# Attention inside a two-layer block: the values become the stationary operand, and the result comes out transposed

## The reference

```python
s_win = jnp.einsum('bnqgrd,bnkgd->bngrqk', qb, kw) * scale
s_win = jnp.where(valid[None, :, None, None], s_win, NEG_INF)
s_ctx = jnp.einsum('bnqgrd,bcgd->bngrqc', qb, k_ctx) * scale
p = softmax(concatenate([s_win, s_ctx, s_sink], -1))
o = einsum(p[..., :kw_len], vw) + einsum(p[..., kw_len:-1], v_ctx)
x = x + g1 * (jnp.concatenate([att, ret, cnv], axis=-1) @ w_out[l])
```

## Time and profile before

| What | Value |
|---|---|
| Median of three runs | 1928.89 us |
| Time of the profiled execution | 1920.56 us |
| Its span, first to last instruction | 1918.8 us |
| PE busy | 1819.8 us (95%) |
| PEld busy | 1482.6 us (77%) |
| DVE busy | 1340.3 us (70%) |
| ACT busy | 1053.6 us (55%) |
| Mean granted PE clock | 0.98 |
| Attention rounds of layer 0 | from about 174 to 266 us |
| Attention rounds of layer 1 | from about 787 to 843 us |

### The profile page before, as it was taken

One profiled execution on the slowest core, in us unless ns is written; L12 is line 12 of the kernel. 1 busy time (PEld: TensorE's weight loads), 2 busy tenths in 40 slices (PEclk: granted clock), 3 DMA queues, 4 the chain that ended last, 5 costly groups with the idle time before them and its releaser, 6 DMA issues.

```text
span 1918.8 us, 23772 instructions
## 1 busy us (share of the span) xinstructions
PE 1819.8 (95%) x8964; PEld 1482.6 (77%) x8964; DVE 1340.3 (70%) x1280; ACT 1053.6 (55%) x1009; POOL 119.8 (6%) x126
## 2 busy tenths in 40 slices
PE   4999999999999999887999999999999999999997
PEld 1886477888888878566788887888888888888885
DVE  2477745432432357755889888889988898889886
ACT  2333643322122244455677667777767777677773
POOL 1032800000000012310000000000000000000000
PEclk9999899999999999998999999999999999999999
DMA  8334833522433134643999998999989999899993
GB/s 290 104 110 145 306 120 88 143 83 82 110 89 104 40 115 140 230 174 132 342 337 377 363 369 306 371 352 362 391 307 363 357 370 378 304 364 363 360 375 141
DMA packets 245911, 472.85 MB, mean 246 GB/s; under 512 B 10546, under 2 KB 60564, under 8 KB 245804
## 3 DMA queue, kind: packets, MB, share of 16 engines
q1 hardware_dynamic: 241712, 468.14, 68.5%
q10 hardware_dynamic: 4092, 3.20, 0.5%
HBM read 470.26 MB, written 1.05 MB: 246 GB/s over the span
## 4 chain that ended last, share of the span: by engine, by line
PE 79%; DVE 7%; DMA 5%; ACT 4%; issue 2%; POOL 2%; SPq 0%; DVEq 0%; ACTq 0%; POOLq 0%
PE bank L543 23%; PE bank L545 23%; PE bank L544 23%; DMA raw<-in_moe_w_gate_dram 2%; DVE parts L1707 2%; PE bank L1047 2%; DMA raw<-in_ada_w_dram 1%; PE bank L561 1%; ACT parts L1410 1%; DMA raw<-in_moe_w_up_dram 1%; PE bank L1102 1%; POOL gb L1663 1%; PE bank L790 1%; DVE parts L1692 1%; ACT parts L1271 1%
## 5 line engine op out<-in xcount | busy, mean ns | idle before, releaser
L1707 DVE TENSOR_TENSOR parts<-raw,parts 128x2048 fp32r<-128x2048 f32 x336 | 764.5, 2288 | 100.8 <-ACT parts L1410 99.7
L1410 ACT ACTIVATE parts<-raw 128x2048 fp32r<-128x2048 f32 x336 | 642.9, 1919 | 236.9 <-DMA raw<-in_moe_w_up_dram 77.0
L543 PE MATMUL bank<-parts,XEr 128*128 128x512 f32 x896 | 355.5, 397 | 7.6 <-DVE parts L1707 5.5
L545 PE MATMUL bank<-parts,XEr 128*128 128x512 f32 x896 | 349.7, 390 | 0.0
L544 PE MATMUL bank<-parts,XEr 128*128 128x512 f32 x896 | 349.1, 390 | 0.0
L1271 ACT ACTIVATE parts<-raw 128x2048 fp32r<-128x2048 f32 (+1 forms) x62 | 113.2, 1831 | 273.4 <-PE bank L545 252.5
L1692 DVE TENSOR_TENSOR parts<-raw,parts 128x2048 fp32r<-128x2048 f32 (+1 forms) x62 | 135.7, 2193 | 143.0 <-ACT parts L1271 142.7
L543 PEld LDWEIGHTS bank<-parts,XEr 128*128 128x128 f32 x896 | 168.6, 188 | 44.5 <-issue 6.2
L545 PEld LDWEIGHTS bank<-parts,XEr 128*128 128x128 f32 x896 | 168.3, 188 | 36.2
L544 PEld LDWEIGHTS bank<-parts,XEr 128*128 128x128 f32 x896 | 168.6, 188 | 33.2
L543 PE MATMUL bank<-parts,HTr 128*128 128x512 f32 x448 | 174.8, 390 | 0.0
(11 more groups left out here) (245 smaller groups left out, 2296.4 us busy)
## 6 DMA issues: line engine op xcount, KB each, us to landing
raw<-in_moe_w_gate_dram SPq DMA_DIRECT2D x112, 1024.0 KB, 6.6
raw<-in_moe_w_up_dram SPq DMA_DIRECT2D x112, 1024.0 KB, 6.6
raw<-in_moe_w_down_dram SPq DMA_DIRECT2D x112, 1024.0 KB, 6.3
raw<-in_ada_w_dram SPq DMA_DIRECT2D x28, 1024.0 KB, 7.9
more<-in_ada_w_dram SPq DMA_DIRECT2D x20, 1024.0 KB, 7.5
raw<-in_w_in_dram SPq DMA_DIRECT2D x12, 1024.0 KB, 5.1
raw<-in_ffn_w_gate_dram SPq DMA_DIRECT2D x22, 512.0 KB, 4.0
raw<-in_ffn_w_up_dram SPq DMA_DIRECT2D x22, 512.0 KB, 5.4
```

Of the source, the lines that this page charges most:

```text
L543: nc.tensor.matmul(out, st[0], mv[0], start=start, stop=False)
L545: return nc.tensor.matmul(out, st[1], mv[0], start=False, stop=stop)
L1410: nc.scalar.activation(parts[:, n % PARTS, 0, :], raw[:, r, :], ACT.Copy).then_inc(hi_ready, 1)
L1707: return nc.vector.tensor_tensor(out, a, b, op)
```

## The change

`values` now takes a pair of heads at once. The stationary operand is the 64 columns of values of one group, the moving one the 128 columns of the transposed probabilities. Group 0 writes partitions 0 to 63 of `OB` and group 1 partitions 64 to 127, alternating from key block to key block. The result has head dims on partitions and tokens on columns, which is what the output projection needs, so `turn_attended` goes away. The row sums still have tokens on partitions. `spread_sums` therefore multiplies each head's inverted sums, broadcast to 64 columns, with the identity (eight f32 matmuls for a tile) into an `AB` bank; ACT copies this to `proj` (`sums_out`), and DVE multiplies `OB` by it (`normalise`).

The order moves with it. `spread_sums` stands on PE in rounds 5, 9, 13 and 17, between `values` and the modulation products. `sums_out` stands on ACT in the following round, behind its exponentials, and `normalise` on DVE in that round, behind the negated maximum (for the last tile in round 17). In rounds 6, 10 and 14 PE does the modulation products ahead of `values`. `attended_high` and `mix_low` read the tile from `proj`, no longer from a bank. The rows of the first half of `w_out` are loaded in another order, by two loads of 64 partitions for each item instead of one of 128. The diff, with indentation cut:

```diff
--- before.py
+++ after.py
@@ -317,6 +317,7 @@
 sarg_ready, esink_ready = sem("sink_arg_ready"), sem("sink_exp_ready")
+recip_ready = sem("row_sums_inverted")
 att_done, att_read = sem("attention_products"), sem("attention_evacuated")
@@ -367,6 +368,10 @@
+def evacuated(layer, i):
+    return layer * (NT + 1) + i + 2
 def attention_of(layer):
@@ -427,10 +432,12 @@
     for h in range(2):
-        for k0, k1 in HALVES:
-            split_item([cols(io["w_out"][layer], h * SLICE, (h + 1) * SLICE, k0, k1)],
-                       k1 - k0, SLICE, n % 2, (n + layer) % 2)
-            n += 1
+        w = io["w_out"][layer][:, h * SLICE:(h + 1) * SLICE]
+        groups = [w[256 * g:256 * g + 256, :].rearrange("(r p) n -> p r n", p=HEAD_DIM) for g in range(KV_HEADS)]
+        split_item(groups, KT // 2, SLICE, n % 2, (n + layer) % 2)
+        n += 1
+        split_item([cols(w, 0, SLICE, KT // 2, KT)], KT // 2, SLICE, n % 2, (n + layer) % 2)
+        n += 1
     if layer == 0:
@@ -750,12 +757,18 @@
-    def turn_attended(layer, t):
-        b = open_mix(layer, t, 0)
-        for i in range(4):
-            c = C_Q + i * P
-            mm = nc.tensor.transpose(b[:, i * P:(i + 1) * P], proj[:, t, c:c + P], ident)
+    def spread_sums(layer, i):
+        t = order_of(layer)[i]
+        mixed[layer, t, 0] = len(mixed) + 1
+        b = open_a(("sums", layer, t))
+        after(recip_ready)
+        turn = i % 2
+        for r in range(4):
+            for g in range(KV_HEADS):
+                head = g * 4 + r
+                mm = nc.tensor.matmul(b[64 * g:64 * g + 64, r * P:(r + 1) * P],
+                                      rsum[:, turn, head:head + 1].broadcast_to([P, HEAD_DIM]), ident, start=True, stop=True)
         mm.then_inc(a_full, 1)
@@ -779,18 +792,19 @@
-        def values(n):
-            t, r, g = its[n]
-            head = g * 4 + r
-            if n % 8 == 0 and n:
+        def values(m):
+            t, r, _ = its[2 * m]
+            if m % 4 == 0 and m:
                 after(att_read)
-            pe.wait_ge(a_done, job[("probs", layer, n)] + 1)
             first = 0 if t < TT else TT
+            pe.wait_ge(a_done, job[("probs", layer, 2 * m + 1)] + 1)
             for kb in range(first, NT):
-                mm = nc.tensor.matmul(OB[:, head * 64:(head + 1) * 64], PT[:, n % 4, kb * P:(kb + 1) * P],
-                                      proj[:, kb, C_V + 64 * g:C_V + 64 * g + 64],
-                                      start=(kb == first), stop=(kb == NT - 1))
-            mm.then_inc(att_done, 1)
+                for g in range(KV_HEADS):
+                    mm = nc.tensor.matmul(OB[64 * g:64 * g + 64, r * P:(r + 1) * P], proj[:, kb, C_V + 64 * g:C_V + 64 * g + 64],
+                                          PT[:, (2 * m + g) % 4, kb * P:(kb + 1) * P],
+                                          start=(kb == first), stop=(kb == NT - 1))
+                    if kb == NT - 1:
+                        mm.then_inc(att_done, 1)
@@ -801,11 +815,13 @@
             if m >= 2:
-                values(2 * m - 4)
-                values(2 * m - 3)
-            if m % 4 == 2 and 6 <= m < last:
-                turn_attended(layer, order_of(layer)[m // 4 - 1])
-            if m < last:
+                if m % 4 == 2 and m < last:
+                    for _ in range(ADA_ITEMS[layer][m]):
+                        ada_product()
+                values(m - 2)
+            if m % 4 == 1 and m >= 5:
+                spread_sums(layer, m // 4 - 1)
+            if m < last and m % 4 != 2:
                 for _ in range(ADA_ITEMS[layer][m]):
@@ -865,7 +881,6 @@
                             after(att_read)
-                            turn_attended(layer, tiles[-1])
                         if i == len(tiles) // 2 - 1:
@@ -1208,6 +1223,9 @@
         for j, src in enumerate(srcs):
+            if src.shape[0] == HEAD_DIM:
+                sp.dma_start(dst[j * HEAD_DIM:(j + 1) * HEAD_DIM, :, :], src).then_inc(raw_loaded[s], 16)
+                continue
             sp.dma_start(dst[:, :, j * part_w:(j + 1) * part_w], src).then_inc(raw_loaded[s], 16)
@@ -1353,6 +1371,13 @@
+    def attended_high(layer, i):
+        t = order_of(layer)[i]
+        act.wait_ge(att_read, evacuated(layer, i))
+        nc.scalar.activation(hTr[:, 0, 0:4, t * P:(t + 1) * P],
+                             proj[:, t, C_Q:C_RQ].rearrange("p (k n) -> p k n", k=4), ACT.Copy).then_inc(mix_hi, 1)
     def mix_high(t, half):
@@ -1371,6 +1396,9 @@
             ins.then_inc(product, 1)
+        def sums_out(i):
+            copy_out(proj[:, order_of(layer)[i], C_Q:C_RQ], take()[:, :])
@@ -1387,6 +1415,8 @@
                     nc.scalar.activation(esink[:, turn, :], esink[:, turn, :], ACT.Exp).then_inc(esink_ready, 1)
+            if m % 4 == 2 and m >= 6:
+                sums_out(m // 4 - 1)
             if m >= 1:
@@ -1397,9 +1427,10 @@
             if m % 4 == 2 and 6 <= m < last:
-                mix_high(order_of(layer)[m // 4 - 1], 0)
+                attended_high(layer, m // 4 - 1)
             if m == last - 1:
                 split_to(first["out", layer] + 2)
+        sums_out(last // 4 - 1)
@@ -1549,7 +1580,7 @@
         nc.scalar.activation(gates, CV[:, 0:nt, :], ACT.Silu).then_inc(act_mix, 1)
-        mix_high(order_of(layer)[-1], 0)
+        attended_high(layer, nt - 1)
         for t in order_of(layer):
@@ -1990,6 +2021,13 @@
         rest, norm = readout(layer), conv_norm(layer)
+        def normalise(i):
+            tile = order_of(layer)[i]
+            dve.wait_ge(att_done, base + 8 * i + 8)
+            dve.wait_ge(a_done, job[("sums", layer, tile)] + 1)
+            tt(proj[:, tile, C_Q:C_RQ], OB[:, :], proj[:, tile, C_Q:C_RQ], ALU.mult).then_inc(att_read, 1)
         dve.wait_ge(conv_gone, CONV_OUTS * (layer + 1))
@@ -2012,6 +2050,8 @@
                     tt(esink[:, turn, :], negm[:, turn, :], sink[:, :], ALU.add).then_inc(sarg_ready, 1)
+                if m % 4 == 2 and m >= 6:
+                    normalise(m // 4 - 1)
                 for c in taps_in(layer, m):
@@ -2027,20 +2067,18 @@
                 turn = (m // 4 - 1) % 2
-                tile = order_of(layer)[m // 4 - 1]
                 after(esink_ready)
                 step(tt(rsum[:, turn, :], rsum[:, turn, :], esink[:, turn, :], ALU.add))
-                step(nc.vector.reciprocal(rsum[:, turn, :], rsum[:, turn, :]))
-                dve.wait_ge(att_done, base + 2 * m - 2)
-                tt(proj[:, tile, C_Q:C_RQ].rearrange("p (h d) -> p h d", d=HEAD_DIM), OB[:, :].rearrange("p (h d) -> p h d", d=HEAD_DIM),
-                   per_group(rsum[:, turn, :], HEAD_DIM), ALU.mult).then_inc(att_read, 1)
+                nc.vector.reciprocal(rsum[:, turn, :], rsum[:, turn, :]).then_inc(recip_ready, 1)
+            if m == last + 1:
+                normalise(last // 4 - 1)
         assert next(rest, None) is None and next(norm, None) is None
     def mix_low(layer, t, half):
-        b = a_bank[full[("mix", layer, t, half)]]
+        b = a_bank[full[("mix", layer, t, half)]] if half else proj[:, t, C_Q:C_RQ]
         k, tok = slice(4 * half, 4 * half + 4), slice(t * P, (t + 1) * P)
         dve.wait_ge(mix_hi, mixed[layer, t, half])
-        tt(hTr[:, 1, k, tok], b[:, :].rearrange("p (k n) -> p k n", k=4), hTr_f[:, 0, k, tok], ALU.subtract)\
+        tt(hTr[:, 1, k, tok], (b[:, :] if half else b).rearrange("p (k n) -> p k n", k=4), hTr_f[:, 0, k, tok], ALU.subtract)\
             .then_inc(mix_lo, 1)
```

## The result

| Kernel | Median, us | Runs | Ratio to the kernel before, same chip |
|---|---|---|---|
| before | 1928.95 | 4 | |
| changed | 1950.05 (1945.37 to 1958.62) | 4 | 1.0111 [1.0087, 1.0135] |
| changed, second time | 1951.77 (1943.32 to 1956.85) | 6 | 1.0128 [1.0100, 1.0156] |

The change makes the kernel slower by 21.1 us in the first comparison. I had said slower, by 9.3, with 1947 as the upper end of the range: the sign held and so did the waits as the main cause, but the sum came to less than half of what was measured. The profiled execution of the changed kernel took 1949.91 us (span 1948.0, granted clock 0.973), that of before 1920.56 (1918.8, 0.980).

What follows compares the result with a forecast made beforehand. PE was taken as busiest, but its new waits for DVE and ACT as deciding: layer 0 +7.2 and layer 1 +2.1 make +9.3 us, put on the median 1928.9: 1938 us, range 1926 to 1947.

Steps and rivals of the forecast that it cites:

- the waits: PE's new waits for DVE and ACT around `spread_sums` and `values` decide: slower, 1933 to 1944 us, chance 0.58.
- A pair of values at 0.97: `values` of two heads on PE: 8 slots of 0.12 us, 0.97 us in place of 1.93.
- Round 11 with `turn_conv` at 5.69: Layer 0, round 11, no new wait: PE's round takes 5.11 + 0.58 us, before 6.25.
- The second meeting: Rounds 6, 10, 14: `values` wait for `normalise`, which ends 5.5 us into the round.
- Round 13 at 4.68 + 1.17 + 1.86: Layer 0, round 13: reciprocal at 4.68 us, then spreading 1.17 and two modulation products 1.86, before round 14.
- The 9.3 us to the maxima of round 15: Layer 0, from round 14's start: DVE does `normalise` until 5.5 us, then `conv_norm`, 3.81 us, before these maxima.
- Layer 1 at +2.1: Layer 1's attention: new waits in rounds 5 and 6 and the tail make it 2.1 us slower.
- The rival of halves that don't overlap: `values` and spreadings on PE take 16 slots, their column halves not running side by side: 1949 us, chance 0.07.
- PE's saving: Rival: the waits cost nothing and PE's shorter work decides, about -5 us, 1924 us, chance 0.13.
- "nothing": Rival: over the whole kernel waits and savings cancel, 1925 to 1933 us, chance 0.13.
- The clock: Rival: stalls in rounds 10, 13, 14 bring PE to half clock, at most +5 us, 1943 us, chance 0.07.
- the first meeting: Rounds 5, 9, 13: `spread_sums` waits for the reciprocal, holding up modulation products and next scores; 0.6 us idle in round 9.

Runs made afterwards that it cites:

- the one with the low half moved: Changed kernel with `mix_low` of layer 0's first attended tile moved from round 7 to round 11: 1948.98 us, ratio 1.0108.
- the fillers: Changed kernel with idle f32 matmuls in layer 0 ahead of the four spreadings and the transposes of rounds 7 to 9: 1946.87 us, ratio 1.0094.
- new form alone: Changed kernel without spreading, `sums_out` or multiplication; DVE copies `OB` out, modulation products behind `values` again, division left out: 1927.81 us, ratio 1.0016.
- neither meeting: Changed kernel, DVE copying `OB` out, spreading one round later, multiplying from the sums' bank, products behind `values`, no ACT copy: 1935.34 us, ratio 1.0034.
- fillers and low half: Changed kernel with both the idle matmuls in layer 0 and the first tile's `mix_low` moved to round 11: 1941.58 us, ratio 1.0065.

## Why the prediction was right in sign and wrong in size

**What held.** A pair of values at 0.97: 1.02. Round 11 with `turn_conv` at 5.69: 5.55. The second meeting 5.5 us into the round: 5.8 in round 10 and 5.55 in round 14. Round 13 at 4.68 + 1.17 + 1.86 = 7.71: 7.72, with PE idle ahead of the spreading for 1.66 us (1.6 expected; in round 9 it was 1.90 in place of 0.6). The 9.3 us to the maxima of round 15, behind `conv_norm`: 9.36. Layer 1 at +2.1: +2.9 on average, which a scatter of 3.8 us between two profiles of one kernel neither confirms nor denies. The rival of halves that don't overlap is out (1.51 when they are made not to), PE's saving doesn't decide, and neither does "nothing".

The Trainium skill ("TensorEngine Tiling (Array Packing)", Performance Considerations) recommends the swap for a moving side of 64 columns, and the Overview of the same page gives up to 2x for it. For the products the trace agrees, 1.93 to 1.02; for the kernel, that form alone gave a ratio of 1.0016.

**Where it failed: layer 0 up to round 10**, where the sum had round 10 at 227.3, 53.3 us after round 0. It came at 58.7, 5.4 later. Of the 11.8 us by which the sum fell short of the medians, 6.9 are layer 0's up to the projection (14.1 and not 7.2). The rest lies in layer 1 (0.8) and in parts for which the sum had nothing: about 1 to 3 us in the dense part and 2.5 to 6 in the experts'; its cause is open. Up to round 10 two steps failed.

*"`attended_high` and `mix_low` do the same size from SBUF as from a bank: nothing."* For `mix_low` it is 4.02 - 2.33 = 1.7 us, when GpSimd works at the same time. From 206.58 to 222.11 GpSimd added without a break, nine additions of 1.73 us. In the kernel before, `mix_low` from the bank took 0.68 in the middle of this and the next instruction 1.69; without `mix_low` that next one took 2.29 alone; with it read from SBUF, 1.77 and 2.29. So the bank version cost DVE nothing: it ran while the next one would have had to wait. The Trainium skill states the rule that I should have weighed ("SBUF — State Buffer", section "SBUF: two separate sides"): a DVE instruction with two SBUF inputs and a GpSimd instruction that reads SBUF exclude each other for a whole instruction. The trace agrees: the excess of 1.09 us is less than one addition of 1.73, and in round 11, with GpSimd idle, it is gone.

GpSimd in the changed kernel, its additions of that stretch in one row:

```profile
206.58 15.53 POOL L1694 TENSOR_TENSOR gb<-gb,QK 128x512 f32<-128x512 f32 x9
```

*The clock.* I priced it as a rival at 0.07 and took full speed for the sum: "the new stalls in rounds 10, 13 and 14". I looked for it behind the stalls that I had found in layer 0's second half, and not behind the first meeting in rounds 5 and 9, where PE also stands still for 2.94 and 1.90 us first. In round 5 it cost 3.77 - 2.02 = 1.75 us from the spreading to the scores of round 6 (changed kernel against the one with the low half moved, which had full speed there), and the readout got all of it: it starts 35.4 us after round 0, and 33.6 at full speed (34.05 in before). In round 9 it cost (1.90 + 3.57) - (1.17 + 1.86) = 2.4 us, with no cover.

The ledger of the 5.4 us: clock in round 5 +1.8, clock in round 9 +2.4, low half from SBUF +1.7, the negated maximum of round 9 +0.5 (1.23 against 0.71), a rest of 0.3; against them the readout's slip of 0.9, which without the clock would have been -0.4, so -1.3. The experiments have the low half at 1.8 and the clock of round 9 at 2.4, after the fillers' own time. Round 5 gained nothing by the fillers (round 6 at 30.5 us with them, at 30.2 without), as the clock had already been at half in round 1 there and the reciprocal came 1.4 us later.

A third term was too small. From round 10 to the projection the sum had +5.1 and the trace has +6.6. Up to the maxima of round 15 it was right (+4.4 against +4.3); the tail came to +2.3 where I had +0.7. The last spreading starts 0.15 us after the end of the reciprocal and takes 1.90 at half clock, and only then can the projection start. In the kernel before it started 0.25 us ahead of the end of the reciprocal. The 1.1 us that I took off, for the transposes saved and for the low clock used up, can only come behind this point, where the next stretch has +0.5 and -1.0. The timeline of PE in the changed kernel, end of layer 0's attention, and the first matmul of the projection in before:

```profile
275.49 1.09 PE L803 MATMUL bank<-PT,proj 128*64 128x128 f32 x16 [3.37 <-ACT PT L1352]
278.25 1.97 PE L770 MATMUL bank<-const,rsum 128*64 128x128 f32 x16 [1.67 <-DVE rsum L2072]
280.15 0.80 PE L550 MATMUL bank<-parts,hTr 128*128 128x512 f32 x1
```
```profile
266.97 0.79 PE L543 MATMUL bank<-parts,hTr 128*128 128x512 f32 x1
```

**What stays open.** The 18.6 and 19.2 us at the gather leave 2.5 to 6 of the measured difference (21.1 and 25.3 between medians) for the experts' part. That the profiles show 11 to 14 there is partly which executions were profiled: those of before took 8.4 and 4.7 us less than the median, those of the changed kernel 0.1 less and 5.1 more. The windows of its first 100 us, in before and in the changed kernel:

```profile
895.60:995.60 100.00, 93.00 (x424) 77.64 (x425) 85.47 (x73) 66.23 (x49) 0.00 (x0) 0.96 0.87 321
```
```profile
913.30:1013.30 100.00, 93.37 (x412) 77.97 (x413) 82.55 (x71) 63.36 (x48) 0.00 (x0) 0.92 0.85 307
```

At 0.92 in place of 0.96, 93 us of PE time would be some 4 us longer, an estimate from these two rows. The difference isn't the changed kernel's alone. Here are stretches with the same code in all versions (one profile each, before and changed two), and the mean granted clock of all executions:

| Version | dense part up to layer 1, us | experts' part, us | clock in its first 100 us | clock, all executions |
|---|---|---|---|---|
| before | 498.3, 498.3 | 1023.2, 1023.1 | 0.96, 0.96 | 0.977 |
| new form alone | 499.4 | 1027.5 | 0.93 | 0.974 |
| neither meeting | 501.4 | 1033.4 | 0.92 | 0.973 |
| changed | 499.5, 501.3 | 1034.7, 1037.4 | 0.92, 0.93 | 0.971 |
| changed, fillers | 502.1 | 1028.6 | 0.94 | 0.975 |
| fillers and low half | 502.1 | 1024.7 | 0.94 | 0.975 |

Every version with the new form is slower there than both profiles of before, also the one without any new wait. Why the clock differs, when the code is the same, no run tells, and no experiment on it was made; and the clock's share, some 4 us, doesn't cover the 11 to 14 either. This is also the open part of the 6 us of the version without meetings.

## What to carry to other kernels

A shorter matmul form is worth what the round's longest chain lets through: here 16 us of PE time came to 2 in layer 0 and to nothing at the end. Before moving a division behind a matmul, count the handovers: with the next scores queued behind a matmul that awaits a reciprocal, the kernel took 9 us more than with the same matmul placed one round later. When a sum has a new PE wait in a critical round, price what follows it at half clock as well, and when an operand moves from a bank to SBUF, look at what GpSimd does at that moment.

## What the runs showed of the hardware that was not expected

Idle matmuls can make the stretch behind a wait shorter: with them, PE got from the end of round 9's reciprocal to round 10 in 3.4 us and not 5.6. They didn't make this kernel measurably faster (1.0094 [1.0077, 1.0111] against 1.0111 [1.0087, 1.0135]), and by round 12 the gain was gone: the clock had fallen at the next wait without a filler, of 2.52 us in round 10. Where the granted clock falls depends on small shifts: in two versions with the same work up to round 6 it fell to 0.83 from 186 to 196 or to 0.68 from 196 to 202, 1.7 us apart at round 6. In round 1, where no edit acts, it was at half in the kernel before and in the version with fillers (0.51 and 0.50), and at full speed in the changed kernel. A DVE instruction of 512 columns with both inputs in SBUF took 0.69 us with GpSimd idle and 1.77 beside its additions; with one input in a bank, 0.68 beside them.
